# Gate products of an expert layer as two float32r products each, with new places for splits and one-hots

## What is computed

```
x = x + merged @ w_out                       # block 1: two recurrent mixers, merged
h = rmsnorm(x, norm_ffn_w)
q = h @ w_q                                  # 8 heads x 2 halves x 128
s = q . sub_keys                             # 128 scores per half; top 16 of each half
expert = the best 16 of the 16 x 16 sums     # 8 heads x 16 choices a token
gates = softmax(best scores)
x = x + sum over choices: gate * gelu(u[expert] . h) * v[expert]     # 128 x 128 experts
x = rmsnorm(x, final_norm_w)                 # end of block 1
h = rmsnorm(x, norm1_g); proj = h @ w_in_2   # block 2
mixed = [rg_lru | stick_breaking attention | diff_attention]
x = x + mixed @ w_out_2;  then a gated feed-forward and a last norm
```

## Time and profile before

| | us |
|---|---|
| median of 3 runs | 3219.65 |
| lowest, highest | 3218.98, 3224.73 |
| the profiled execution | 3222.15 |
| its span, first to last instruction | 3219.9 |
| mean granted clock of PE over the span | 0.993 |
| PE, POOL, DVE, ACT busy | 97%, 72%, 53%, 26% |

### The profile page before, as it was taken

The page is one execution under the profiler, slowest core; times in us unless marked ns, Lnnn a source line. Parts: engine busy times, 40 slices in busy tenths (PEclk is TensorE's granted clock), DMA queues, the critical chain, the costliest instruction groups (busy, mean ns, idle before and its releaser), DMA issues.

```text
span 3219.9 us, 41721 instructions
## 1 busy us (share of the span) xinstructions
PE 3127.2 (97%) x14246; PEld 2525.5 (78%) x14246; DVE 1695.1 (53%) x2491; ACT 822.7 (26%) x1405; POOL 2332.7 (72%) x1127
## 2 busy tenths in 40 slices
PE   7999999999999999999999999999999998799998
PEld 6788777888888888888888888888888775578886
DVE  6488644221246443353443366667676567676621
ACT  3244123210112333333334211111111254332211
POOL 6834654677776888888887788888888763278876
PEclk9999999999999999999999999999999999899999
DMA  3211211223323344434444666666666421022222
GB/s 141 92 52 46 98 66 59 85 95 121 106 97 107 119 171 176 159 134 176 171 170 151 225 183 187 191 190 188 182 188 190 133 79 40 20 92 95 95 98 72
DMA packets 245543, 405.66 MB, mean 126 GB/s; under 512 B 145600, under 2 KB 145728, under 8 KB 244160
## 3 DMA queue, kind: packets, MB, share of 16 engines
q1 hardware_dynamic: 224560, 331.68, 32.6%
q10 hardware_dynamic: 20880, 72.62, 5.8%
HBM read 335.04 MB, written 69.21 MB: 126 GB/s over the span
## 4 chain that ended last, share of the span: by engine, by line
PE 91%; DVE 4%; ACT 2%; issue 1%; POOL 1%; DMA 0%; ACTq 0%; POOLq 0%; SPq 0%; DVEq 0%
PE bank L590 23%; PE bank L592 23%; PE bank L591 23%; PE banks L590 2%; PE banks L592 2%; PE banks L591 2%; PE bank L887 2%; PE banks L736 1%; PE bank L801 1%; PE banks L887 1%; PE bank L702 1%; PE bank L700 1%; PE bank L701 1%; ACT hot L1274 1%; PE banks L700 1%
## 5 line engine op out<-in xcount | busy, mean ns | idle before, releaser
L497 POOL TENSOR_TENSOR w_hi<-w_raw,ones 128x1024 fp32r<-128x1024 f32 x492 | 956.4, 1944 | 756.3 <-PE bank L592 630.4
L499 POOL TENSOR_TENSOR w_lo<-w_raw,w_hi 128x1024 fp32r<-128x1024 f32 x492 | 1230.0, 2500 | 38.6
L590 PE MATMUL bank<-h_hi,w_hi 128*128 128x512 f32 x2176 | 865.5, 398 | 9.7 <-DVE h_lo L1867 7.1
L592 PE MATMUL bank<-h_hi,w_lo 128*128 128x512 f32 x2176 | 848.3, 390 | 0.0
L591 PE MATMUL bank<-h_lo,w_hi 128*128 128x512 f32 x2176 | 847.9, 390 | 0.0
L590 PEld LDWEIGHTS bank<-h_hi,w_hi 128*128 128x128 f32 x2176 | 409.3, 188 | 105.3 <-DVE h_lo L1867 13.9
L592 PEld LDWEIGHTS bank<-h_hi,w_lo 128*128 128x128 f32 x2176 | 408.8, 188 | 86.6
L591 PEld LDWEIGHTS bank<-h_lo,w_hi 128*128 128x128 f32 x2176 | 409.3, 188 | 82.0 <-issue 2.4
L2328 DVE TENSOR_TENSOR ew_lo<-expert_w,ew_hi 128x512 fp32r<-128x512 f32 x128 | 249.1, 1985 | 182.0 <-ACT ew_hi L1583 178.2
L2276 DVE TENSOR_TENSOR hot<-bank,tab 128x512 f32<-128x512 f32 x224 | 137.0, 681 | 361.4 <-PE banks L887 358.5
L590 PE MATMUL bank<-ew_hi,w_hi 128*128 128x512 f32 x768 | 303.6, 395 | 0.0
(11 more groups left out here) (434 smaller groups left out, 4163.3 us busy)
## 6 DMA issues: line engine op xcount, KB each, us to landing
w_raw<-weights SPq DMA_DIRECT2D x494, 512.0 KB, 3.7
acts<-act_out_stage ACTq DMA_DIRECT2D x128, 256.0 KB, 2.8
gates<-gate_stage ACTq DMA_DIRECT2D x8, 4096.0 KB, 13.2
acts_in<-acts SPq DMA_DIRECT2D x128, 256.0 KB, 4.3
gates_in<-gates SPq DMA_DIRECT2D x128, 256.0 KB, 4.7
resid<-x SPq DMA_DIRECT2D x4, 512.0 KB, 8.3
resid<-x ACTq DMA_DIRECT2D x4, 512.0 KB, 8.0
out<-final SPq DMA_DIRECT2D x3, 512.0 KB, 2.7
```

The lines of the kernel that those rows point to most:

```text
L497: nc.gpsimd.tensor_tensor(w_hi[:, pair, :], w_raw[:, slot, :], one_col.to_broadcast((P, 1024)), ALU.mult).then_inc(hi_split, 1)
L499: nc.gpsimd.tensor_tensor(w_lo[:, pair, :], w_raw[:, slot, :], f32(w_hi[:, pair, :]), ALU.subtract).then_inc(split_done, 1)
L590: mm(out_, hi, rhs_hi, start=first, stop=False)
L592: return mm(out_, lo, rhs_hi, start=False, stop=last)
```

## The change

`LOT_TILES` becomes (4, 4, 4, 4, 3, 3, 3, 2). `hot1`, `hot2` and a new `hot1_lo` are float32r; the gate of a choice is split on DVE into a float32r high part and a low part, and four arrays are turned. DVE makes both hots of all four batches and the product of `hot1` (not yet gated) with the low gate, read from the turned bank; POOL multiplies `hot1` by the high gate. PE makes two float32r products a token, both with `hot2` as weights. POOL gates the next step's first batch after up to three splits of this one, then makes the rest of the splits, then gates the other three. ACT's share of the hots, with its semaphores, goes. In the sweep the sum is written to the PSUM bank, both parts are made from there, add and low part alternate, and ACT copies the sum back to the residual. In block 2 POOL's splits of the output tiles wait for mixed parts or weights, `lru_out(0)` stands behind `df_maps(1, 3)` and the weights, and the output parts are in another order.

```diff
-LOT_TILES = (4, 4, 4, 4, 4, 4, 2, 1)
+LOT_TILES = (4, 4, 4, 4, 3, 3, 3, 2)
...
# POOL
+        def gate_batch(step, p):
+            pool.wait_ge(hot_ready, c.due(hot_ready, 3))
+            first = (step % (LOTS * STEPS) * HOTS + p) * TOKENS_PER_BATCH
+            gate = gates_t[:, first:first + TOKENS_PER_BATCH]
+            nc.gpsimd.tensor_tensor(hot1[:, p], f32(hot1[:, p]), gate.unsqueeze(2).to_broadcast((P, TOKENS_PER_BATCH, NKEYS)),
+                                    ALU.mult).then_inc(hot_gated, 1)
...
+        for p in range(HOTS):
+            gate_batch(0, p)
+        for step in range(TT * LOTS * STEPS):
+            n = LOT_TILES[step // STEPS]
+            early = min(n, 3)
+            splits(early)
+            tile += early
+            for p in range(HOTS if step + 1 < TT * LOTS * STEPS else 0):
+                gate_batch(step + 1, p)
+                if p == 0:
+                    splits(n - early)
+                    tile += n - early
...
             if p == 0:
                 pool.wait_ge(sb_z_done, TT * SB_HEADS)
+                pool.wait_ge(mixed_ready, MIXED[3])
             else:
                 pool.wait_ge(df_s_done, TT * DF_HEADS)
+                pool.wait_ge(sb_w_ready, SB_HEADS)
...
+        pool.wait_ge(mixed_ready, MIXED[1])
         split(0)
         split(1)
         held_split(0)
...
# PE
             pe.wait_ge(split_done, c.due(split_done))
+            if in_banks:
+                pe.wait_ge(h_ready, c.due(h_ready, 0) + 1)
+                pe.wait_ge(plain_hi, c.due(plain_hi, 0) + 3)
...
-            for n in range(3):
+            for n in range(4):
                 ins = nc.tensor.transpose(bank[6 + tt % 2][:, n * P:n * P + P], chosen[:, n, :], t_("identity"))
...
                 pe.wait_ge(hot_gated, c.due(hot_gated))
-                if p == HOTS - 1:
-
-                    pe.wait_ge(last_hot, c.due(last_hot))
                 pe.wait_ge(gate_read, c.due(gate_read, 1, back=HOTS))
                 for t in range(TOKENS_PER_BATCH):
-                    ins = mm(bank[2 + p][:, t * P:t * P + P], hot2[:, p, t, :], hot1[:, p, t, :],
-                             start=t == 0, stop=t == TOKENS_PER_BATCH - 1)
+                    mm(bank[2 + p][:, t * P:t * P + P], hot2[:, p, t, :], hot1[:, p, t, :], start=t == 0, stop=False)
+                    ins = mm(bank[2 + p][:, t * P:t * P + P], hot2[:, p, t, :], hot1_lo[:, p, t, :],
+                             start=False, stop=t == TOKENS_PER_BATCH - 1)
...
         df_spread(1)
+        out_part(0, 5)
+        out_part(1, 5)
+        out_part(2, 5)
         out_part(2, 3)
-        for k in (6, 0, 1, 2, 3):
+        out_part(3, 6)
+        out_part(3, 0)
+        out_part(0, 7).then_inc(tile_done, 1)
+        out_part(1, 7).then_inc(tile_done, 1)
+        out_part(2, 7).then_inc(tile_done, 1)
+        for k in (1, 2, 3, 5):
             out_part(3, k)
-        for n in range(4):
-            out_part(n, 5)
-        for n in range(4):
-            out_part(n, 7).then_inc(tile_done, 1)
+        out_part(3, 7).then_inc(tile_done, 1)
...
# ACT: of gate_batches only the four evictions are left
-            for t in range(TOKENS_PER_BATCH):
-                fn_at(hot2[:, p, t, :], t_("iota128"), ACT.Abs, scale=-1.0,
-                      bias=chosen_t[:, 1, bass.ds(first + t, 1)]).then_inc(hot_distance, 1)
-            act.wait_ge(hot_distance, c.due(hot_distance, TOKENS_PER_BATCH))
-            c.alone()
-            fn_at(hot2[:, p], hot2[:, p], ACT.Relu, scale=-1.0, bias=ones[:, 0:1]).then_inc(last_hot, 1)
...
+        def sum_back(k):
+            act.wait_ge(h_ready, LOWS + k + 1)
+            fn(resid[:, k, :], bank[k][:], ACT.Copy).then_inc(act_step, 1)
         for k in range(KT):
             act.wait_ge(x_added, c.due(x_added))
-            plain_part(k, gains[:, k:k + 1])
+            fn(h_hi[:, k, :], bank[k][:], ACT.Copy, scale=gains[:, k:k + 1]).then_inc(plain_hi, 1)
+            if k:
+                sum_back(k - 1)
+        sum_back(KT - 1)
+        act.wait_ge(act_step, c.due(act_step, KT))
...
# DVE
+            gate_hi_part = chosen[:, 2, :].bitcast(F32R)
+            ts(gate_hi_part, chosen[:, 3, :], 1.0, None, ALU.mult).then_inc(dve_step, 1)
+            dve.wait_ge(dve_step, c.due(dve_step))
+            tt_(chosen[:, 3, :], chosen[:, 3, :], f32(gate_hi_part), ALU.subtract).then_inc(chosen_done, 1)
...
-                for key, hot in ((1, hot2), (0, hot1)) if p < HOTS - 1 else ((0, hot1),):
...
+                for key, hot in ((1, hot2), (0, hot1)):
+                    tt_(hot[:, p], tokens[key], t_("iota128").unsqueeze(1).to_broadcast(big), ALU.is_equal).then_inc(hot_ready, 1)
+                dve.wait_ge(hot_ready, c.due(hot_ready, 2))
+                tt_(hot1_lo[:, p], f32(hot1[:, p]), tokens[3], ALU.mult).then_inc(hot_ready, 1)
...
-            tt_(resid[:, k, :], resid[:, k, :], bank[k][:], ALU.add).then_inc(x_added, 1)
+            tt_(bank[k][:], resid[:, k, :], bank[k][:], ALU.add).then_inc(x_added, 1)
+
+        def sweep_low(k):
+
             dve.wait_ge(x_added, c.due(x_added))
+            dve.wait_ge(plain_hi, c.due(plain_hi))
+            stt(h_lo[:, k, :], bank[k][:], gains[:, k:k + 1], f32(h_hi[:, k, :]), ALU.mult, ALU.subtract).then_inc(h_ready, 1)
...
         for k in range(4):
             sweep_added(k)
-        for k in range(4):
-            plain_low(k, gains[:, k:k + 1])
+            if k:
+                sweep_low(k - 1)
         for k in range(4, KT):
...
             sweep_added(k)
-        for k in range(4, KT):
-            plain_low(k, gains[:, k:k + 1])
+            sweep_low(k - 1)
+        sweep_low(KT - 1)
...
                 df_maps(h, 2)
-                if h == 1:
-                    lru_out(0)
                 df_maps(h, 3)
                 sb_weights(h)
                 if h == 1:
+                    lru_out(0)
                     lru_out(1)
```

More of the change, by code:

```diff
@@ L44 @@
 LOT_BATCHES = STAGED_TOKENS // TOKENS_PER_BATCH
+STEPS = LOT_BATCHES // HOTS
 KEY_SLOTS = 4
@@ L524, in _ @@
         tile += LEAD_TILES
-        for lot in range(TT * LOTS):
-            if LOT_TILES[lot] % RAW == 0:
-                def mixed(i):
-                    gate_batches(lot, i)
-                    splits(LOT_TILES[lot])
-                c.repeat(LOT_BATCHES // HOTS, mixed)
-                tile += LOT_BATCHES // HOTS * LOT_TILES[lot]
-            else:
-                for i in range(LOT_BATCHES // HOTS):
-                    gate_batches(lot, i)
-                    splits(LOT_TILES[lot])
-                    tile += LOT_TILES[lot]
+        for p in range(HOTS):
[10 more added lines that the diff above has]
+                    tile += n - early
+            if step + 1 == TT * LOTS * STEPS:
+                splits(n - early)
+                tile += n - early
         tail = START["experts"] + NKEYS - tile
@@ L666, in plain_fm, with fresh_fm @@
             return before
-        def fresh_fm(n, plain, sum_after, read, also_read=0, late_sum=None):
-            before = plain_fm(plain, sum_after)
+        def fresh_fm(n, plain, sum_after, read, also_read=0, late_sum=None, in_banks=False):
+            before = plain_fm(plain, sum_after, in_banks)
             c.due(read, also_read)
@@ L905, in mixed @@
                         turn(next_choices)
+            next_choices = (lot + 1) // LOTS if lot % LOTS == LOTS - 1 and lot + 1 < TT * LOTS else 0
             if LOT_TILES[lot] % 2:
-                for i in range(its):
-                    mixed(i * LOT_TILES[lot])
-            else:
-                c.repeat(its - 1, lambda i: mixed())
-                mixed(0, (lot + 1) // LOTS if lot % LOTS == LOTS - 1 and lot + 1 < TT * LOTS else 0)
+                for i in range(STEPS):
+                    mixed(i * LOT_TILES[lot], next_choices if i == STEPS - 1 else 0)
+            else:
+                c.repeat(STEPS - 1, lambda i: mixed())
+                mixed(0, next_choices)
         tiles_fm(NKEYS - LEAD_TILES - LOT_BATCHES // HOTS * sum(LOT_TILES), h_hi, h_lo, acc_read_act)
@@ L2272, in one_hots @@
                 big = (P, TOKENS_PER_BATCH, NKEYS)
-                for key, hot in ((1, hot2), (0, hot1)) if p < HOTS - 1 else ((0, hot1),):
-                    of = turned_keys[:, key * P + first:key * P + first + TOKENS_PER_BATCH]
-                    tt_(hot[:, p], of.unsqueeze(2).to_broadcast(big),
-                        t_("iota128").unsqueeze(1).to_broadcast(big), ALU.is_equal).then_inc(hot_ready, 1)
+                tokens = [turned_keys[:, n * P + first:n * P + first + TOKENS_PER_BATCH].unsqueeze(2).to_broadcast(big) for n in range(4)]
+                for key, hot in ((1, hot2), (0, hot1)):
+                    tt_(hot[:, p], tokens[key], t_("iota128").unsqueeze(1).to_broadcast(big), ALU.is_equal).then_inc(hot_ready, 1)
+                dve.wait_ge(hot_ready, c.due(hot_ready, 2))
+                tt_(hot1_lo[:, p], f32(hot1[:, p]), tokens[3], ALU.mult).then_inc(hot_ready, 1)
```

(7 more changed lines are left out.)

49 lines of the change are left out of this document (19 added, 30 removed).

## The result

The changed kernel runs in 3181.62 us, the median of four runs (3179.26 to 3183.49), against 3220.90 for the kernel before on the same chip: ratio 0.9874, 95% interval 0.986 to 0.9889. The forecast was 3181.0, with a range of 3166 to 3199. The profiled execution took 3179.26 with a span of 3177.4, so the span fell by 42.5 us (from 3219.9).

A forecast was written before the change was run, and what follows sets the result against it. PE, busy 97% of the span, was taken as the bound, so only its waits or own work count. Terms -28.0, +0.4, -2.3, -6.3 and -2.8 sum to -39.0, from 3219.65 to about 3181 us, range 3166 to 3199.

The forecast's parts named there:

- The two products: Gate steps: two float32r products cost the same 0.1117 us each as the fp32 records they replace; 0, bounds -56 and +119.
- Rivals 1 and 2: Gate products: 0.057 us each, bound by the stream, 3125 us, 6%; or 0.228 each whatever the width, 3300 us, 4%.
- ScalarE's hot: Gate steps: PE's 0.74 us wait for ScalarE's last hot goes in 32 steps, plus 4.0 behind a store; -28.0 us.
- the transposes' 0.4: Gate part: the fourth transpose adds 4 x 0.11 us to PE; +0.4.
- VectorE's extra work: Gate steps: twelve hot operations instead of seven, VectorE ending 20.5 us into the longest step, covered by the tiles.
- under 10 us into each step: Sign to look for in the gate steps: twelve hot operations of 0.68 us end within this time.
- POOL between the splits: Gate steps: POOL's splits and gatings fit PE's step, the split behind the gatings ready over 1 us early; cost 0.
- Sweep: Residual sweep: add and low part alternate at 1.44 us a pair, PE's first tile ends earlier; -2.3 us, bounds 0 and -3.5.
- Attention: Second block's attention part: POOL's splits moved and the map put ahead of lru_out(0); -6.3 us, bounds 0 and -12.
- The new contention: Attention part: POOL's splits behind lru_out(1) fall on the next head's softplus, which ends 4.6 to 4.8 us later.
- Merge: Output tiles of the second block: PE's 2.81 us idle before the fifth tile goes; -2.8 us, bounds 0 and -3.
- Rival 3 (the clock falls): Gate part: clock falls costing 1.2 to 1.7 us each, 32 of them 38 to 54, giving 3219 to 3235 us; 3%.

The follow-up runs named there:

- e1: The changed kernel with each token's gate product as one fp32 product again, the gate's low part left out: 3180.19 us, ratio 0.9872.
- e3: The changed kernel with the one-hots and both gate parts in bfloat16 instead of float32r, still two products a token: 3136.12 us, ratio 0.9738.
- e4: The changed kernel with the last hot2 of each step built by ScalarE again, so PE waits for it: 3231.25 us, ratio 1.0031.
- e7: The kernel of e4 with one fp32 product a token in place of the two float32r ones: 3215.78 us, ratio 0.998.
- e5: The changed kernel with the tiles per step of before, (4, 4, 4, 4, 4, 4, 2, 1): 3188.31 us, ratio 0.9897.
- e2: The changed kernel without the product with the low hot, so one float32r product a token: 3138.78 us, ratio 0.9749.
- e6: The changed kernel with POOL's four gatings behind the first split of a step instead of the third: 3441.21 us, ratio 1.0682.
- the two versions that missed: Built on e3: gate in three or two bfloat16 parts, POOL gating two by two, last lots 3, second output split later: 3183.84 and 3147.57 us.
- e9: The changed kernel without POOL's three new waits ahead of the output splits, the map still ahead of lru_out: 3184.03 us, one execution.
- e8: The changed kernel with its whole second block undone (sweep, lru_out, POOL's waits, order of output parts): 3192.65 us, ratio 0.991.

## Why the prediction was right

The sum was -39.0 and each of its terms was found where it was put. That 3181.0 met 3181.6 so closely is luck: the medians moved by 39.3, but the two profiled spans by 42.5, of which 0.6 is chance ahead of the gates, and three terms hold misses that cancel or that something covered.

- **The two products, 0.** Right, and shown by e1. The pitch taken from the loads, 0.1117, is 0.110. Rivals 1 and 2 (0.057 or 0.228 a product) are out for float32r. The load as the bound is shown by the pitch staying at 0.11 while the columns alone ask 0.057. A pitch of 0.055 exists, but it comes with the type of the load (e3), which I had not listed.
- **ScalarE's hot, -28.0.** Right in place and size for this change: 26.6 in the gate parts and 29.5 in the stage, the transposes' 0.4 included. What I had not seen is that the term is not the wait's alone. Put back into the changed kernel, the wait costs 50 (e4), and with fp32 products 34 (e7). Without this part the change as a whole would have been 10 us slower than the kernel before (e4).
- **VectorE's extra work, 0.** The cost is right, the working is not. The hots are done 8.8 into an ordinary step (9.6 forecast), but the longest step ends at 24.2 and not at 20.5, because the choice behind them is held beside POOL; this was left out. The sign "under 10 us into each step" fails in two three-tile steps (12.1 and 15.4) and in those with a turn (17.8). Nothing reached PE, with as little as 1.4 us to spare. e5 shows what the cover is worth once it is gone.
- **POOL between the splits, 0.** Right, though the split behind the first gating is ready 0.4 to 0.7 us before PE needs it in the four-tile steps that I read, not over 1, and the sum per step that I gave for it is not the argument that decides. e2, e3, e6 and the two versions that missed all show that it is the place of a gating between the splits.
- **Sweep, -2.3.** Mis-sized: -3.5, at my bound. Add and low part alternate at 1.26 a pair, not 1.44, and the clock did not fall, so the first tile ends at 2529.7, about 12.6 after the first add, where I had 13.3.
- **Attention, -6.3.** -5.8, out of three misses. PE's transposes start 6.4 earlier (1.4 and 4.9 forecast) with an idle of 1.67, as said. The head's end comes only 8.1 earlier, not 9.5: the clock was not full, 0.80 over the 8.4 us from the transposes on. The new contention was on the softplus, but with 2.8 more rather than 4.6 to 4.8: the first split was over when the softplus began, and only one POOL split met it. At its end 5.4 are left, and the masking adds 0.5 of its 1.6. e9 gives POOL's waits 3.7 of the gain and the moved lru_out the rest.
- **Merge, -2.8.** -3.1 in the trace, 3.0 in e8; the idle left is 0.15.
- **Rival 3 (the clock falls).** It did not happen, but e4 shows that it was near: idle of 0.74 beside float32r products was enough in seven of 32 steps, for about 1.6 us each, inside the price of 1.2 to 1.7. The same change takes the idle away.

The change does what it says, and its second block is worth 11 to 15 of the 39 to 42 us (e8).

## What to carry to other kernels

Where short products wait for their weights, count loads and look at what type they are loaded in, not at passes or columns: two float32r products cost what one fp32 product does (0.22 us), and three bfloat16 ones less than either (0.17). An engine that prepares data for another by turns is judged by where each piece stands in its queue relative to the consumer, not by its sum per step: the same gatings cost 0 behind the third split and 260 us behind the first. And float32r pairs in place of fp32 products came free only where the short waits beside them went too (e4, e7): make the two edits together. Last, work on VectorE is priced by what POOL does at that time, not by its mean.

## What the runs showed that I had not expected

- **A short wait and float32r pairs brought the clock down together, neither alone.** 0.74 us of idle a step: with fp32 products 1.00 and 26.1 us (e7, and the kernel before), with float32r pairs of the same pitch 0.94 and 27.7 us in six of the four-tile steps (e4); pairs without the wait 1.00 in all 32 steps. A long wait does it with either product: 0.88 behind the store of before, 0.93 in e7, 0.90 in e6.
- **float32r weights are loaded like fp32 ones, bfloat16 weights twice as fast.** A load of 128x128 shows 0.19 and starts 0.11 behind the last one for fp32 and float32r, 0.10 and 0.055 for bfloat16.
- **POOL held no VectorE operation that reads an input from PSUM.** Beside the splits the sweep's adds and low parts stay at 0.69 and 0.75 us, and all 256 comparisons at 0.68 to 0.69. With inputs in SBUF alone the softplus goes from 1.69 to 4.45 for its four operations, and the choice's from 0.2 to 0.4 up to 1.9 to 2.6. A result that goes to PSUM does not help: L2249 writes a bank and takes 2.00 instead of 0.43.
